# Scores of four K pages in one product of 512 columns, eight page buffers, and another order of a stage's first loads

## The reference, cut to what matters

```python
rev = lax.cumsum(lp32, axis=1, reverse=True) - lp32          # forget sums of the past rows
lg_past = einsum('bqhd,bkhd->bhqk', q, k_past) * scale + cn_t[..., :, None] + rev_t[..., None, :]
lg_new  = einsum('bqhd,bkhd->bhqk', q, k) * scale + cn_t[..., :, None] - cn_t[..., None, :]
p = softmax(concatenate([lg_past, lg_new], axis=-1))
return einsum('bhqk,bkhd->bqhd', p[..., :past], v_past) + einsum('bhqk,bkhd->bqhd', p[..., past:], v)
```

## Time and profile before

| what | us |
|---|---|
| median of 3 runs (lowest, highest) | 5930.59 (5924.33, 5937.43) |
| the profiled execution's own time | 5919.57 |
| its span in the trace | 5917.9 |
| TensorE matmul busy, whole span | 4521.1 |
| VectorE busy, whole span | 3140.7 |
| the changed stage in the trace | 1513 to 2461 |

### The profile page before, as it was taken

How to read it: one execution, slowest core, us unless ns; L and a number is a source line. 1 busy time by engine, 2 the same in 40 slices (tenths; PEclk the granted TensorE clock), 3 DMA queues, 4 the chain that set the end, 5 groups by cost and what they waited for, 6 DMA issues and landing times. The chain is left out here.

```text
span 5917.9 us, 56343 instructions
## 1 busy us (share of the span) xinstructions
PE 4521.1 (76%) x22069; PEld 3385.3 (57%) x22069; DVE 3140.7 (53%) x4358; ACT 644.4 (11%) x981; POOL 1647.2 (28%) x1721
## 2 busy tenths in 40 slices
PE   8999999999488889799999979999899960000000
PEld 7999999999456666577537745555555530000000
DVE  2322222222355565300011069697969779998888
ACT  2211212212112112000001000000000000000000
POOL 0000000000343443100000012222222247777775
PEclk9999999999789899899999989999999985555555
DMA  3333232322565666622334479999999989999998
GB/s 142 118 117 106 101 106 99 105 105 71 145 221 195 222 205 198 234 101 88 139 121 136 157 286 413 421 406 419 420 421 420 421 353 406 410 401 384 373 382 336
DMA packets 342314, 1465.41 MB, mean 248 GB/s; under 512 B 86564, under 2 KB 117204, under 8 KB 202184
## 3 DMA queue, kind: packets, MB, share of 16 engines
q0 software_dynamic: 177888, 995.21, 43.0%
q1 hardware_dynamic: 133432, 435.05, 20.4%
q10 hardware_dynamic: 30768, 32.11, 1.6%
HBM read 1366.90 MB, written 94.75 MB: 247 GB/s over the span
## 5 line engine op out<-in xcount | busy, mean ns | idle before, releaser
L2021 DVE SCALAR_TENSOR_TENSOR i_acc<-i_row,i_cf,i_acc 128x2048 f32<-128x2048 f32 x571 | 1344.8, 2355 | 201.5 <-DMA i_row<-in_expert_v,i_ei 144.2
L1828 PE MATMUL i_p_h<-i_xT,i_ut 128*128 128x384 f32 x4096 | 1332.6, 489 | 38.0 <-DMA i_ut<-in_u_tiles 30.6
L1828 PEld LDWEIGHTS i_p_h<-i_xT,i_ut 128*128 128x128 f32 x4096 | 782.5, 191 | 585.8 <-DMA i_ut<-in_u_tiles 32.5
L2137 POOL DMA_INDIRECT i_row<-in_expert_v,i_ei x576 | 581.1, 1009 | 632.9 <-DVE i_acc L2021 464.5
L233 PE MATMUL a_acc<-a_xh,a_wh 128*128 128x288 f32 x3104 | 672.3, 298 | 28.8 <-DVE a_wl L456 24.6
L233 PE MATMUL a_acc<-a_xh,a_wl 128*128 128x288 f32 x3104 | 665.5, 296 | 0.0
L233 PE MATMUL a_acc<-a_xl,a_wh 128*128 128x288 f32 x3104 | 665.1, 296 | 0.0
L233 PEld LDWEIGHTS a_acc<-a_xh,a_wh 128*128 128x128 f32 x3104 | 499.7, 189 | 40.3 <-issue 35.2
L233 PEld LDWEIGHTS a_acc<-a_xh,a_wl 128*128 128x128 f32 x3104 | 500.9, 189 | 0.0
L233 PEld LDWEIGHTS a_acc<-a_xl,a_wh 128*128 128x128 f32 x3104 | 500.8, 189 | 0.0
L2012 DVE CUSTOM_DVE_ANT_0 i_row<-i_row,i_acc 128x2048 f32<-128x2048 f32 x192 | 432.3, 2285 | 103.9 <-DMA i_row<-in_expert_u,i_ei 101.8
(11 more groups left out here) (271 smaller groups left out, 4022.7 us busy)
## 6 DMA issues: line engine op xcount, KB each, us to landing
i_ut<-in_u_tiles SPq DMA_DIRECT2D x128, 1024.0 KB
a_w<-in_w_in SPq DMA_DIRECT2D x97, 1024.0 KB, 4.8
f_wo<-in_w_out SPq DMA_DIRECT2D x32, 1024.0 KB, 5.0
f_wq<-in_w_query SPq DMA_DIRECT2D x32, 1024.0 KB, 5.2
tmp_uT<-a_out POOLq DMA_DIRECT2D x97, 288.0 KB, 2.4
tmp_Ha<-i_ho ACTq DMA_DIRECT2D x128, 192.0 KB
f_low<-in_w_bs SPq DMA_DIRECT2D x16, 1024.0 KB, 5.8
c_csb<-tmp_cs SPq DMA_DIRECT2D x32, 288.0 KB
```

Of the source, the lines that this page charges most:

```text
L1828: last = nc.tensor.matmul(p_h[:, e % 2, 0:ND], ut[:, e % 4, k * P:(k + 1) * P], xT[:, k, :], start=(k == 0), stop=(k == KT - 1))
L2021: v.scalar_tensor_tensor(acc, row[:, m % R, :], cf[:, j, k:k + 1], acc, ALU.mult, ALU.add).then_inc(row_used, 1)
L2137: pool.indirect_dma_start(row[:, m % R, :], None, table, bass.IndirectOffsetOnAxis(index, axis=0)).then_inc(row_in[m % R], 16)
```

## The change

Six things change, all in `mamba_and_samples`. K gets eight page buffers instead of six; POOL's order above is unchanged in the code but depends on RK. A scores block waits for all of its four pages, then makes eight products of 512 columns, each over the same 128 partitions' slice of four neighbouring buffers, and counts its four pages as used together at the end. The scaled output `ov` has no buffer of its own any more; it is a view of the first two quarters of `pr`. The taps `gc` get a semaphore of their own, and VectorE waits for it alone before the convolutions of group 0; it waits for the other constants (now 128 = 8 loads) after the forget sums. SyncE's first loads are reordered: after `load_raw(0)` and `gc` come `load_new(0)`, `ident`, `tf` and the other constants, and `load_group(0)` follows behind them.

```diff
-    RK, RV = 6, 4
+    RK, RV = 8, 4
...
         pr = sb("e_pr", [P, 4, 512])
+        ov = pr[:, 0:2, :].rearrange("p a n -> p (a n)")
...
-        ov = sb("e_ov", [P, DA])
...
+        gc_in = tl.sem("c_gc_in")
...
                 load_raw(0)
-                sp.dma_start(gc[:, :, :], io["group_par"].rearrange("g p n -> p g n")).then_inc(const_in, 16)
+                sp.dma_start(gc[:, :, :], io["group_par"].rearrange("g p n -> p g n")).then_inc(gc_in, 16)
+                load_new(0)
+                sp.dma_start(ident[:, :], io["ident"]).then_inc(const_in, 16)
                 sp.dma_start(tf[:, :, :], dr["facg"].rearrange("g p n -> p g n")).then_inc(const_in, 16)
-                load_group(0)
-                for dst, src in ((ident, "ident"), (mask_p, "mask_st"), (mask_s, "mask_ss"), (seqm, "seqm"), (ones, "ones"),
+                for dst, src in ((mask_p, "mask_st"), (mask_s, "mask_ss"), (seqm, "seqm"), (ones, "ones"),
                                  (sel, "sel_hq"), (maskn, "mask_new")):
                     sp.dma_start(dst[:, :], io[src]).then_inc(const_in, 16)
-                load_new(0)
+                load_group(0)
                 load_v(0)
...
                 conv_edges(0)
-                dve.wait_ge(const_in, 144)
+                dve.wait_ge(gc_in, 16)
                 for a in range(4):
                     conv(0, a)
                 query(0)
                 forget_sums(0)
+                dve.wait_ge(const_in, 128)
...
-                    for c in range(4 * u, 4 * u + 4):
-                        m = PAGES * b + c
-                        pe.wait_ge(k_in[m % RK], 16 * (m // RK) + 16)
-                        for j in range(8):
-                            last = nc.tensor.matmul(bank[:, (c % 4) * PAGE:(c % 4 + 1) * PAGE], qp[:, j * P:(j + 1) * P],
-                                                    kr[:, m % RK, j * P:(j + 1) * P], start=(j == 0 and c % 4 == 0), stop=False,
-                                                    skip_group_check=True)
-                        last.then_inc(k_used, 1)
-                    nc.tensor.matmul(bank, sel[:, :], rev[:, 512 * u:512 * u + 512], start=False, stop=True,
-                                     skip_group_check=True).then_inc(s_out, 1)
+                    m = PAGES * b + 4 * u
+                    for i in range(m, m + 4):
+                        pe.wait_ge(k_in[i % RK], 16 * (i // RK) + 16)
+                    for j in range(8):
+                        last = nc.tensor.matmul(bank.rearrange("p (c n) -> p c n", n=PAGE), qp[:, j * P:(j + 1) * P],
+                                                kr[:, m % RK:m % RK + 4, j * P:(j + 1) * P], start=(j == 0), stop=False)
+                    last.then_inc(k_used, 4)
+                    nc.tensor.matmul(bank, sel[:, :], rev[:, 512 * u:512 * u + 512], start=False, stop=True).then_inc(s_out, 1)
...
-                pe.wait_ge(const_in, 144)
+                pe.wait_ge(const_in, 128)
```

More of the change, by code:

```diff
@@ L1156, in _ @@
                     act.wait_ge(o_out, g + 1)
-                    nc.scalar.mul(ov[:, :], e_ps[:, 0:2, :].rearrange("p a n -> p (a n)"), st[:, 11:12]).then_inc(oc_out, 1)
+                    nc.scalar.mul(ov, e_ps[:, 0:2, :].rearrange("p a n -> p (a n)"), st[:, 11:12]).then_inc(oc_out, 1)
                     if g < 7:
```

## The result

Six runs of each kernel: before 5926.22 us (5920.91 to 5937.43), after **5984.37 us** (5980.93 to 5988.9). The ratio is 1.0097, 95% interval 1.0084 to 1.011: **58 us slower**, where I forecast 5835 and gave faster a chance of 0.84. The forecast was wrong, in its sign too. The profiled execution of after has a span of 5981.5 us, 63.6 more than before's.

The account below looks back on a forecast made before the run. The changed stage was taken as bound by TensorE's fixed list plus what it waits for. Terms: -106 - 6 + 22 + 6 - 12 = -96, giving 5823.6 us profiled, 5835 on the median's scale; range 5805 to 5905.

Parts of the forecast that it names:

- Step 1, the stalls: Groups 0 to 6's first halves: fewer scores products end TensorE's stalls; -106 us, bounds 0 and -112.
- The rival that I gave 0.09: The stalls have another cause, such as forget gathers or next group's loads: +10, 5941 us, no difference; chance 0.09.
- "remote" wait: VectorE's wait after short products, 114.7 us in 14 pieces, two per group in seven groups; forecast to be gone.
- Step 2, width: Scores blocks: sixteen products of 512 columns are quicker than 64 narrow ones; -6 us, bounds 0 and -9.
- Step 3, values wait: TensorE waits longer for V page 8, behind eight K pages instead of six; +22 us, bounds +17 and +38.
- Step 4, whole-block waits: Scores: four pages must land before a block's first product; 1 us in six groups, +6, bounds 0 and +36.
- just in time: Fourth scores block: page 15, issued at 24.4 us, lands at 30.6; the block starts at about 30.7.
- My slower rival: Block waits decide, at the last scores block in groups 1 to 6: +60, 5991 us; chance 0.07.
- Step 5, start: Stage start: VectorE waits for the taps alone, so the first scores block comes earlier; -12 us, bounds -8 and -15.
- Step 6: Output in the exponentials' buffer: the needed orders of writing and reading already stand, so nothing is added.

Follow-up runs that it names:

- block_wait: Kernel before with eight page buffers, output in the exponentials' buffer, scores waiting for and releasing four pages at once, products still narrow: 6036.1 us, ratio 1.0185.
- old_start: Changed kernel with the old order of the stage's first loads: 5996.6 us, ratio 1.0118.
- pause: Changed kernel with forget gathers 8 to 15 of the next sample waiting for the fourth block of scores: 5853.6 us, ratio 1.0120.
- reordered: Changed kernel; next group's loads wait for fourth scores block, group 1's raw lines earlier, next K pages spread behind V pages 7, 11, 15: 5917.6 us, ratio 0.9992.
- before_again: Kernel before, unchanged, run again on a chip of the faster kind: 5777.6 us, ratio 1.0001.
- after_again: Changed kernel, as it is, run again on a chip of the faster kind: 5828.0 us, ratio 1.0069 to the kernel before.
- no_forgets_third: Changed kernel without the forget gathers of samples 1 to 7, on a chip of the slower kind: 5835.7 us, ratio 0.9850.

## Why the prediction was wrong

*Step 1, the stalls (-106; measured, on A: +48 in the first halves of passes 0 to 6).* This is the step that failed. The observation was right, that the halves with the forget gathers have 112 us of excess over the last, and two thirds of it do stand in TensorE's blocks of scores. The reading was not: that TensorE's own instructions, "about 18 instructions (loads and products) per us", overfill "something on TensorE's issue or signalling path". Instructions and signals of TensorE are indeed what is late; what brings it on are the forget gathers. The rival that I gave 0.09, "the gathers of forgets or the loads of the next group", was right in its first half, and the runs show it: without the forget gathers the excess is gone with the loads in place, without the loads it stays, and with the gathers it moves. (Its time, 5941, was still 43 too low; the buffers below are missing in it.) My evidence against it was weak: "blocks of 512 columns don't suffer" was read from blocks of values, beside which POOL gathers pages and no forgets, and it says nothing of the signals between blocks. In pass 0 after the change blocks of 512 columns do suffer. The "remote" wait of the earlier trace rows, 114.7 us, was the better row, and I used it as a second symptom of the same cause. After the change TensorE's gaps are nearly gone ("issue" in the scores 5.7 us; before it was 45.8) and the end of the half isn't earlier, since it hangs on the signals. Where wide products have no page wait to answer for (block_wait to old_start) they give 40 us: that much of step 1 was real. The rule of the Trainium skill that I set beside that rival (page "Runtime: NRT & Kernel Launch", section "Instruction fetch mechanics") is that the cost of fetching is mostly hidden. The traces agree on B, where fewer instructions bought the width alone, 1.1 us a pass; it does not explain the 40 us on A, where the profile shows no fetch in the gaps of block_wait.

Why it got worse and didn't stay: the kernel before with two more buffers (eight_pages) has it all. Before, POOL stopped in the middle of its run for a free K buffer, and in pass 1 the signals of the third chunk came through in that stop. With eight buffers 28 gathers follow each other (1681 to 1715 us in the changed kernel), the hold has no break, and VectorE's part of that chunk, some 9 us, comes after the release and no longer before it. That the stop of the run is what lets the signals through is read from the traces; the run made for it, pause, fell on B and didn't test it.

*Step 2, width (-6; measured -9).* A block takes 7.03 us, not 7.31; pass 7 is 1.1 us shorter, times eight. Right, at its bound. The remark that the trace's step is "a little wider" than 134 cycles was wrong: 0.1117 us are 268 cycles of 2.4 GHz, twice as many.

*Step 3, values wait (+22; measured +24 on A, +28 on B).* Seven waits, 30.8 us in place of 18.1: second halves 388.9 against 364.6. Right in kind and place. That the sum fits so well is in part luck: the wait grew by 13 us and not by 18, and the other 12 us, for which I had 4, are slower blocks and what else the halves hold. The cure was cheap: reordered has 5.9 us of that wait, and second halves of 341.5.

*Step 4, whole-block waits (+6; bound +36).* The size was wrong. On B, where nothing else covers it, the wait on K pages comes seven times, 25.9 us, 24.9 of it in passes 1 to 6. The blocks behind it are 0.1 to 2.9 us slower, 11 in six, and three first blocks are some 2 us slower each. Together this is the 43 us by which the first halves of passes 1 to 6 exceed six of 44.3. What failed is "just in time". The issue was nearly right: 24.7 to 27.1 us into the half, for 24.4 in the sum. The landing was not: I took 6.2 us from V page 8, beside which SyncE issues no loads, and the last K page took 9.4 to 10.7 with V pages 0 to 3, forgets and the next group's loads beside it; with those loads out of the way it takes 5. My slower rival named this mechanism; on B it is the larger part of the loss, beside the values wait. On A it is hidden in the hold (14.2 us in three passes), so the sum there may not count it again.

*Step 5, start (-12).* The first block starts 10.8 us earlier: right. "load_v(0), load_new(1) and load_group(1) move back by less and are read tens of us later: nothing" was wrong. I did not follow what stands behind group 1's loads on the same queue: the raw lines of group 1, which VectorE now wants earlier in pass 0 and gets later. That is 20.4 us of VectorE's wait, and pass 0 is 10.5 us longer, in part for this. Between 0 and 12 us are left.

*Step 6 (0).* No row speaks against it.

Sum on A by halves, from the profiled executions: start -10.8, first halves of passes 0 to 6 +47.9, second halves +24.3, pass 7 -1.1: +60.3 until the last values, against a stage that is 59 longer.

## What to carry to other kernels

When one half of a loop is slower than its last turn, list everything that the last turn lacks and ask of each which row it explains; here gathers, loads and buffers all differed, and I picked a fourth cause. A wait of one engine for an event whose sender had long been done is a row of its own kind: ask who was busy from the send to the arrival. More prefetch buffers can cost time: what was prefetched stands in front of what is needed now, and, as I read the traces, they let the issuing engine run without the stops in which others got through.

## What the runs showed of the chip

- TensorE's signals are held while POOL issues small gathers back to back, on chips of kind A. Of the 40 signals at the end of a chunk's products in the stage, VectorE stood waiting for this long after the products' end: for 15 in before on A over 1 us, up to 10.6; for 7 in after on A 9.7 to 23.3 us; for none over 1 us in before_again and after_again on B and in no_forgets_third on A. Twelve gathers of K and V pages in the same half cost nothing; with 16 forget gathers of 16 rows among them the half takes 18 to 26 us more (after against no_forgets_third, pass by pass).
- In that time TensorE's own records can come slowly, instead or as well: narrow ones one per 0.7 to 2 us in block_wait, after 40 without a gap; wide ones one per 1.4 to 2.8 us in pass 0 of after, and without a gap in its pass 1.
- Chips differ: 5924 us against 5782 for one program. In the trace of after on A 3 to 9 semaphore events per 3 us are recorded from 1684 to 1720 us and 111 in the next 3; on B 29 to 68 per 3 us in the same part of the pass, 1679 to 1712. Between 1515 and 2300 us 3,678 landings are recorded on A and 8,678 on B, while the gathers' queue has 40,960 packets in the stage on both. So on A events come through at one to three per us while POOL gathers. What makes the chips differ, and whether it is events or something that they share a way with, no run here tells. Nor does one tell whether the recording of the profile takes part: every execution here has a recorded span and clock, and none without recording is there to compare.
- A gather of 128 rows cost POOL 0.95 us, one of 16 rows 0.86: it pays to gather all heads of eight pages at once.
